# Moving the normed activations of a thirteen-layer kernel by 16 bytes in SBUF

## The reference, cut to what matters

```python
def rms_norm(x, g):
    xf = x.astype(jnp.float32)
    y = xf * lax.rsqrt(jnp.mean(xf * xf, axis=-1, keepdims=True) + RMS_EPS)
    return (y * g.astype(jnp.float32)).astype(x.dtype)

def swiglu(x, w_in, w_out):
    gate, up = jnp.split(x @ w_in, 2, axis=-1)
    return (jax.nn.silu(gate) * up) @ w_out
```

## Time and profile before

| | |
|---|---|
| median of 3 runs | 2163.64 us (2162.86 to 2165.47) |
| span of the profiled execution | 2161.0 us |
| TensorE busy | 2126.5 us, 98% |
| VectorE, ScalarE, GpSimd busy | 1607.5, 1307.3, 586.1 us |
| mean granted TensorE clock | 0.998 of full speed |

### The profile page before, as it was taken

How to read it: one execution, slowest core, us unless ns; L and a number is a source line. 1 busy time by engine, 2 the same in 40 slices (tenths; PEclk the granted TensorE clock), 3 DMA queues, 4 the chain that set the end, 5 groups by cost and what they waited for, 6 DMA issues and landing times.

```text
span 2161.0 us, 39632 instructions
## 1 busy us (share of the span) xinstructions
PE 2126.5 (98%) x14203; PEld 1920.3 (89%) x14203; DVE 1607.5 (74%) x1915; ACT 1307.3 (60%) x1815; POOL 586.1 (27%) x450
## 2 busy tenths in 40 slices
PE   8999899999999999999999999999999999999998
PEld 7889899888888899999888888999888888888887
DVE  7875888886887676766887687665887688677874
ACT  6664776664665565665665566475665466456663
POOL 3431672440342000000442243000342144122430
PEclk9999999999999999999999999999999999999999
DMA  6665467666566555554566567544566566534673
GB/s 211 193 199 180 128 191 259 193 209 189 166 194 212 165 172 162 160 160 150 168 194 211 158 194 220 159 145 149 177 192 212 158 191 202 187 108 150 191 221 100
DMA packets 371157, 387.92 MB, mean 180 GB/s; under 512 B 11334, under 2 KB 366031, under 8 KB 371056
## 3 DMA queue, kind: packets, MB, share of 16 engines
q1 hardware_dynamic: 357104, 369.14, 54.9%
q10 hardware_dynamic: 13952, 17.41, 2.5%
HBM read 376.02 MB, written 10.49 MB: 179 GB/s over the span
## 4 chain that ended last, share of the span: by engine, by line
PE 90%; DVE 5%; ACT 3%; POOL 1%; issue 1%; DMA 0%; ACTq 0%; DVEq 0%
PE ps L839 44%; PE ps L840 23%; PE ps L793 3%; PE ps L794 3%; PE ps L795 3%; PE ps L814 2%; PE ps L815 1%; PE ps L816 1%; DVE xg L1742 1%; PE ps L883 1%; DVE wlo L1724 1%; PE ps L885 1%; PE ps L884 1%; PE ps L1056 1%; PE ps L1024 1%
## 5 line engine op out<-in xcount | busy, mean ns | idle before, releaser
L1724 DVE TENSOR_TENSOR wlo<-raw,whi 128x1024 fp32r<-128x1024 f32 (+2 forms) x652 | 883.1, 1364 | 153.7 <-ACT whi L1304 152.6
L839 PE MATMUL ps<-xg,whi 128*128 128x512 f32 x2816 | 981.8, 392 | 4.1 <-DVE xg L1742 1.9
L1304 ACT ACTIVATE whi<-raw 128x1024 fp32r<-128x1024 f32 (+2 forms) x652 | 720.6, 1113 | 190.5 <-PE ps L840 130.2
L840 PE MATMUL ps<-xg,wlo 128*128 128x256 f32 x2816 | 794.5, 282 | 0.0
L839 PEld LDWEIGHTS ps<-xg,whi 128*128 128x128 f32 x2816 | 529.2, 188 | 118.3 <-DVE xg L1742 3.9
L840 PEld LDWEIGHTS ps<-xg,wlo 128*128 128x128 f32 x2816 | 532.9, 189 | 0.2
L839 PE MATMUL ps<-hT,whi 128*128 128x512 f32 x1408 | 488.5, 390 | 0.0
L840 PE MATMUL ps<-hT,wlo 128*128 128x256 f32 x1408 | 397.1, 282 | 0.0
L839 PEld LDWEIGHTS ps<-hT,whi 128*128 128x128 f32 x1408 | 264.3, 188 | 55.4
L2235 POOL TENSOR_TENSOR gate_r<-gate,r 128x512 f32<-128x512 f32 x88 | 189.6, 2155 | 286.5 <-DVE gate L1802 286.5
L840 PEld LDWEIGHTS ps<-hT,wlo 128*128 128x128 f32 x1408 | 266.1, 189 | 0.0
(11 more groups left out here) (286 smaller groups left out, 3067.2 us busy)
## 6 DMA issues: line engine op xcount, KB each, us to landing
raw<-in_ffn_w_in SPq DMA_DIRECT2D x352, 512.0 KB, 3.5
raw<-in_ffn_w_out SPq DMA_DIRECT2D x64, 768.0 KB, 4.7
raw<-in_ffn_w_out SPq DMA_DIRECT2D x64, 640.0 KB, 4.7
raw<-in_w_kv SPq DMA_DIRECT2D x48, 512.0 KB, 3.6
raw<-in_a_w_in SPq DMA_DIRECT2D x32, 512.0 KB, 4.5
raw<-in_b_w_q SPq DMA_DIRECT2D x24, 512.0 KB, 3.8
raw<-in_sb_w_qkv SPq DMA_DIRECT2D x24, 512.0 KB, 3.9
bias_by_distance<-bias_rows ACTq DMA_DIRECT2D x12, 768.0 KB, 5.0
```

Of the source, the lines that this page charges most:

```text
L839: nc.tensor.matmul(out, whi[:, par, w], both, start=first and k == 0, stop=False)
L840: mm = nc.tensor.matmul(out[:, 0:T], wlo[:, par, w], both[:, 0:T], start=False, stop=last and k == total - 1)
L1304: nc.scalar.activation(whi[:, par, off:off + size], raw[:, 2 * par + half, :size], ACT.Copy).then_inc(hi_done, 1)
L1724: nc.vector.tensor_tensor(wlo[:, par, off:off + size], raw[:, 2 * par + half, :size], whi[:, par, off:off + size].bitcast(F32), ALU.subtra ...
```

## The change

`xg` becomes a view into a wider tile. Four float32r columns (16 bytes) lie ahead of it and twelve (48 bytes) behind it, so `xg` begins 16 bytes later, and everything that is allocated behind it 64 bytes later. `raw`, `whi`, `wlo` and `x` stay. No instruction is added, removed or reordered.

```diff
-    xg = sb("xg", [P, KC, 2, T], F32R)
+    xg_room = sb("xg_room", [P, 4 + KC * 2 * T + 12], F32R)
+    xg = xg_room[:, 4:4 + KC * 2 * T].rearrange("p (c s t) -> p c s t", c=KC, s=2)
     xg_hi, xg_lo = [xg[:, :, n, :] for n in range(2)]
```

## The result

Before 2164.20 us (median of 4 runs, 2162.86 to 2165.47), after 2176.48 us (4 runs, 2174.47 to 2178.76); the ratio is 1.0058 with a 95% interval of 1.0045 to 1.0070. The profiled execution of the changed kernel spans 2176.4 us.

A forecast was written before the change was run, and what follows sets the result against it. TensorE, busy 98% of the span, was taken as the bound. 7360 moving reads x 1.7 ns = 12.5 us, other parts costed at nothing or left out: 2163.6 + 12.5 = 2176 us; range 2168 to 2192, all cases from 2150.

The forecast's parts named there:

- TensorE bounds, and a nanosecond per matmul goes into the time one for one: Whole kernel: TensorE busy 98% of the span, so each matmul's change adds directly, except at seams between layers.
- The writers of xg cost nothing: 192 ScalarE and VectorE instructions writing xg: at most 7 ns each, nearly all beside TensorE; costed at nothing.
- The 7360 moving reads: Matmuls with xg as moving operand: 1.7 ns more each from the new distance to the weights, 12.5 us.
- All tiles behind xg, by 64 bytes: hT, xk, attention tiles and constants keep their distances modulo 64 to the weights; costed at nothing.
- The price taken from the stick-breaking sums: Groups at distance 0 modulo 64 seemed 3.9 ns per matmul slower; as upper price 29 us, 2192.
- the first rival: "Nothing happens": the 3.9 ns may come from changing between 256 and 512 columns, not place; 2164 us, chance 0.30.
- The 1.7 ns from the exchanged roles: Three-product helper with weights moving and xg stationary: 0.355 us per triple, 1.7 ns more per matmul, read as another distance.
- Nothing happens: Reads of xg: a whole 16-byte shift splits no read, overhead comes from loading weights; 2164 us, chance 0.30.
- Faster: Moving and weight streams are better parted at 48 than 32: 2151 us, at the floor 2080; chance 0.23.
- Much slower: Starts off a multiple of 32 fetch one piece more, 24.5 us, or break pace, to 1010; above forecast range 0.07.
- The 64 bytes matter: hT and xk streams change as well; no row speaks for it, a small chance inside the cases.

The follow-up runs named there:

- xg16_alone: Against the kernel before: xg 16 bytes further on, xk 64 bytes, constants, hT and the rest unmoved; 2175.31 us, ratio 1.0052.
- all64: Against the kernel before: every tile, weights included, 64 bytes further on, no distance changed; 2163.62 us, ratio 0.9999.
- mix64_all96: Against the kernel before: all tiles 96 bytes on; xg for attention and recurrence layers, xk and those layers' outputs 32 further; 2162.43 us, ratio 0.9995.
- behind64_alone: Against the kernel before: xg unmoved, everything behind it 64 bytes further on; 2169.77 us, ratio 1.0028.
- The kernel of distance 0: Against the kernel before: weights 32 bytes further on, so moving operands lie 0 behind them modulo 128 (before: 32); 2176.48 us, ratio 1.0056.
- the kernels of distance 0 and 64: Weights 32 or 96 bytes further on than before, moving operands 0 or 64 behind them modulo 128; 2176.48 and 2186.17 us.
- distance 48: Against the kernel before: weights 112 bytes further on, so moving operands lie 48 behind them modulo 128; 2180.50 us, ratio 1.0078.
- distance 80: Against the kernel before: weights 80 bytes further on, so moving operands lie 80 behind them modulo 128; 2193.81 us, ratio 1.0137.

## Why the prediction was right, and where it wasn't

Time 2176 forecast, 2176.48 measured; slower forecast, slower by 12.3 us where 12.5 were forecast. That the sum came out so close is in part luck. In the bill of the profiled execution the reads that were costed at 12.5 us took 10.3 (7.0 + 3.3), those that moved by 64 bytes and were costed at nothing 7.4, and the value helper and all else 2.5 less, 15.2 in all where the medians differ by 12.3. Point by point:

*TensorE bounds, and a nanosecond per matmul goes into the time one for one: shown.* The distances add up to 15.2 of 15.4 us.

*The writers of xg cost nothing: right,* 494 and 480 ns.

*"The 7360 moving reads" at 1.7 ns, because of the distance to the weights: that the distance counts is shown, the price was near (10.3 us over 7360 is 1.4 ns), its form was wrong.* `xg16_alone` gives 11.6 us for it, with xk's move in it, where 12.5 were forecast. `all64` and `mix64_all96`, with the runs that moved one side, show that the distance and not the place sets the pace. The rule of the Trainium skill ("SBUF — State Buffer", "Who interferes with whom"), that TensorE's two read ports are independent and it never waits on anyone, leaves no room for this: here one operand's place beside the other's is worth up to 1.4% of the time. Nor was a shift by one whole 16-byte cacheline, as its section Specifications sizes them, free. But the price is no slope between neighbours. A layer's pairs take 346.67, 350.0 or 351.1 ns, at 2.4 GHz 832, 840 or 842.7 cycles, and the forecast's one pace of 350 was that of four of the eight layers only. Triples on xg were forecast at 355 and took 355.0.

*"All tiles behind xg, by 64 bytes. [...] I cost this at nothing": this step failed.* I took the period of 64 for granted; it is 128 for pairs, as near as the runs tell, and more for triples. `behind64_alone` measured the move at 6.0 us, and in the profile after, `hT`, xk and the out-projections carry 4.9 + 1.3 + 1.2 us. 11.6 and 6.0 add up to 17.6, not 12.3. About 1.2 us of that is xk's move, which is in both; in the profiled executions xg's pairs lost 8.6 us in `xg16_alone` and 7.0 in the changed kernel, because their layers fell into other paces. The rest isn't explained.

*The price taken from the stick-breaking sums (3.9 ns at distance 0): refuted.* The kernel of distance 0 should have been at 2190 by it and was at 2176.5. The order of 256 and 512 columns or something else made those rows longer, as the first rival had warned; their operands kept their distances in the changed kernel, and a group took 0.470 us (forecast 0.475). The 1.7 ns from the exchanged roles rests on no better ground. The prediction called it another distance, but by its own count modulo 64 exchanging the roles turns 32 into 32; and in the changed kernel, with xg's streams slower, the value helper's matmuls on xg went from 118.3 to 117.8 ns. The 1.7 ns was of the right size, not of the right cause.

*The rivals.* "Nothing happens" is out by the interval. "Faster" is out for this distance, and no distance tried is faster. "Much slower", by a read that is split off a multiple of 32, isn't needed: the kernels of distance 0 and 64 lose with all operands on a multiple of 32, and at distance 48 the pairs show the same 351.1 ns whether xg or the weights begin off one. The loss of the changed kernel was half of the 24.5 us of that rival. A move of everything by 16 bytes stays untested. "The 64 bytes matter", for which I found no row, was half true, beside the forecast and not in place of it; its sign, that the pairs on `hT` change too, was there.

*Open:* why a matmul costs 16 cycles over its columns (triples at 340 ns) to 40 (pairs at 353.3) and why the number comes in steps; what picks a layer's pace where several are possible; and what the distance modulo 256, or that between `whi` and `wlo`, does to the triples. The experiments show that distance matters, not through which part of the chip.

## What to carry to other kernels

In a kernel bound by back-to-back float32r matmuls, the distance in SBUF between the moving and the stationary operand was worth 0.3 to 1.4% here; a tile inserted anywhere can change it, so a variant that adds or resizes a tile ahead of a matmul's operand should be padded to keep the old distances before its time is read. Modulo 128 was enough for the whole time here, though not for every stream; modulo 256 is the safer guess, and no run tried it. The measure is the distance between starts over a few dozen matmuls, in every layer, not the mean duration. And when one tile's move is costed, cost the move of everything behind it by the same argument.

## What the runs showed of the hardware

- A steady stream of float32r pairs locks into one of a few paces, 346.67, 348.9, 350.0, 351.1, 351.7 or 353.3 ns for 768 columns, and, behind the first eight or sixteen pairs, holds it over the 352 pairs of a layer; the next layer, with the same operands at the same places, may take another (346.7 in the third layer, 351.1 in the fourth, in the profile after).
- The two kernels whose tiles all moved together, by 64 and by 96 bytes, kept their time to 0.1%; the largest loss, at distance 80, was 30 us.
- A move by 128 bytes against the weights left pairs at 346.7 ns but took triples on xk from 350.4 to 354.6.
- The same distance modulo 128 gave most triples of 256-column matmuls 0.340 us in one kernel and 0.353 in another.
